# Gate and up projections by a seven-product (Strassen) form for two of eight pairs of k-tiles per chunk

## The reference, cut to what matters

```python
D_MODEL, SEQ, D_FF = 2048, 256, 5632
def swiglu(h, w_gate, w_up, w_down):
    return (jax.nn.silu(h @ w_gate) * (h @ w_up)) @ w_down
x = x + 0.5 * swiglu(rmsnorm(x, ffn1_norm), ffn1_w_gate, ffn1_w_up, ffn1_w_down)
...   # input projection, HGRN2, sparse attention, output projection, cross attention
x = x + 0.5 * swiglu(rmsnorm(x, ffn2_norm), ffn2_w_gate, ffn2_w_up, ffn2_w_down)
out = rmsnorm(x, final_norm)
```

## Time and profile before

| | |
|---|---|
| median of 3 runs | 2023.91 us (2022.93 to 2025.12) |
| profiled execution: span | 2022.1 us |
| TensorE busy | 2005.9 us, 99% of the span, 10238 matmuls |
| VectorE busy | 1105.0 us, 55% |
| ScalarE busy | 947.7 us, 47% |
| HBM read | 373.14 MB, 186 GB/s over the span |

### The profile page before, as it was taken

The page is one execution under the profiler, slowest core; times in us unless marked ns, Lnnn a source line. Parts: engine busy times, 40 slices in busy tenths (PEclk is TensorE's granted clock), DMA queues, the critical chain, the costliest instruction groups (busy, mean ns, idle before and its releaser), DMA issues.

```text
span 2022.1 us, 26565 instructions
## 1 busy us (share of the span) xinstructions
PE 2005.9 (99%) x10238; PEld 1657.0 (82%) x10238; DVE 1105.0 (55%) x1394; ACT 947.7 (47%) x1201; POOL 13.6 (1%) x19
## 2 busy tenths in 40 slices
PE   9999999999999999999999999999999999999998
PEld 7888888888888888878777888888888888888886
DVE  5544544445445546766658675644454544444444
ACT  6444444444454444455555564644444444444443
POOL 0000000000000000000002000000000000000000
PEclk9999999999999999999999999999999999999999
DMA  8666666666666556665433465566666666655564
GB/s 300 192 188 189 185 192 190 187 188 212 213 194 190 191 175 209 185 188 164 135 125 117 167 202 163 166 189 190 192 188 188 187 189 190 210 189 195 192 195 146
DMA packets 198859, 376.32 MB, mean 186 GB/s; under 512 B 13312, under 2 KB 19712, under 8 KB 198656
## 3 DMA queue, kind: packets, MB, share of 16 engines
q1 hardware_dynamic: 196960, 374.51, 60.4%
q10 hardware_dynamic: 1824, 0.77, 0.1%
HBM read 373.14 MB, written 2.10 MB: 186 GB/s over the span
## 4 chain that ended last, share of the span: by engine, by line
PE 96%; ACT 2%; DVE 1%; DMA 1%; issue 0%; SPq 0%; DVEq 0%; ACTq 0%
PE psum L1558 90%; PE psum L1581 2%; PE psum L1769 1%; PE psum L1812 1%; PE psum L1570 1%; ACT w_hi L518 0%; DVE w_lo L967 0%; DMA w_raw<-in_g 0%; ACT prob L759 0%; PE psum L1782 0%; PE psum L1867 0%; DMA w_raw<-in_w_in 0%; PE psum L1791 0%; ACT silu_gate L759 0%; PE psum L1805 0%
## 5 line engine op out<-in xcount | busy, mean ns | idle before, releaser
L967 DVE TENSOR_TENSOR w_lo<-w_raw,w_hi 128x1024 fp32r<-128x1024 f32 x694 | 848.4, 1225 | 868.4 <-ACT w_hi L518 866.5
L518 ACT ACTIVATE w_hi<-w_raw 128x1024 fp32r<-128x1024 f32 x694 | 734.5, 1060 | 993.3 <-PE psum L1558 969.9
L1558 PE MATMUL psum<-w_hi,xT_hi 128*128 128x512 f32 (+1 forms) x1824 | 712.6, 391 | 1.5 <-DVE w_lo L1084 1.3
L1558 PE MATMUL psum<-w_hi,xT_lo 128*128 128x512 f32 (+1 forms) x1824 | 707.6, 388 | 0.0
L1558 PE MATMUL psum<-w_lo,xT_hi 128*128 128x512 f32 (+1 forms) x1824 | 707.0, 388 | 0.0
L1558 PEld LDWEIGHTS psum<-w_hi,xT_hi 128*128 128x128 f32 x1824 | 342.5, 188 | 71.5 <-issue 1.6
L1558 PEld LDWEIGHTS psum<-w_hi,xT_lo 128*128 128x128 f32 x1824 | 342.4, 188 | 70.8
L1558 PEld LDWEIGHTS psum<-w_lo,xT_hi 128*128 128x128 f32 x1824 | 342.7, 188 | 68.2
L1558 PE MATMUL psum<-w_hi,ffT_hi 128*128 128x512 f32 x784 | 306.4, 391 | 0.0
L1558 PE MATMUL psum<-w_hi,ffT_lo 128*128 128x512 f32 x784 | 305.2, 389 | 0.0
L1558 PE MATMUL psum<-w_lo,ffT_hi 128*128 128x512 f32 x784 | 305.0, 389 | 0.0
(11 more groups left out here) (250 smaller groups left out, 864.8 us busy)
## 6 DMA issues: line engine op xcount, KB each, us to landing
w_raw<-in_u SPq DMA_DIRECT2D x176, 512.0 KB, 3.7
w_raw<-in_d SPq DMA_DIRECT2D x176, 512.0 KB, 4.4
w_raw<-in_g SPq DMA_DIRECT2D x175, 512.0 KB, 3.7
w_raw<-in_w_in SPq DMA_DIRECT2D x88, 512.0 KB, 3.7
w_raw<-in_w_out SPq DMA_DIRECT2D x32, 512.0 KB, 3.6
w_raw<-in_cw SPq DMA_DIRECT2D x8, 512.0 KB, 3.7
w_raw<-in_wk SPq DMA_DIRECT2D x8, 512.0 KB, 4.6
w_raw<-in_wq SPq DMA_DIRECT2D x8, 512.0 KB, 3.6
```

The costliest lines, as they stand in the source:

```text
L518: nc.scalar.activation(w_hi[:, slot], w_raw[:, slot], ACT.Copy).then_inc(w_hi_ready, 1)
L967: nc.vector.tensor_tensor(w_lo[:, slot], w_raw[:, slot], w_hi[:, slot].bitcast(F32), ALU.subtract)\
L1558: mm = nc.tensor.matmul(dst[:, t, 0:width], act_t, w[:, slot, kk, 0:width], start=(first and kk == 0 and n == 0), stop=(last and kk == KT_ ...
```

## The change

**Which products.** In chunks 1 to 10 of each half-step, k-tiles 0, 1 and k-tiles 2, 3 are taken as pairs. With the two token tiles as rows, the two k-tiles as the inner dimension and (gate, up) as columns, a pair is a 2 x 2 by 2 x 2 product of blocks, 8 block products of 3 matmuls each. It is now done by 7 block products (Winograd's variant of Strassen's form). That needs four sums of token blocks (`s_hi`, `s_lo`, made once in each half-step by `token_forms`) and, for each pair and chunk, three sums of weight blocks (`t_f32`, then `t_hi`, `t_lo`) and a fourth that is written over `w_raw`.

**Order.** A unit is now one k-tile with both gate and up columns (the input is laid out anew for this, `gu1`, `gu2`), so that all four of banks 0 to 3 are open through the whole chunk. The pairs are units 0, 1 and 6, 7 (`PAIR_AT`). The first unit of a pair is four block products into banks 4, 6, 7, 5, the second is three block products into banks 0, 1, 2. The other 12 units are 12 matmuls as before (`both_unit`).

**Gathering.** After unit 7 ScalarE copies bank 4 (`p1_copied`) and VectorE combines banks 5 to 7 in three additions into `comb` (`combined`). At the chunk's end VectorE adds banks 0, 1 and then 2, 3 to `comb` (`c_taken`, L1274 of the changed kernel), ScalarE takes silu in `comb`, and VectorE writes the product (`hid_ff`). The transposes of the product before now follow unit 12 (`TURN_H`).

**Memory.** `t_f32`, `t_lo`, `t_hi` and `hid_ff` lie in the memory of `x`. In the first half-step `x` is loaded again from the input during the first down chunk, in four transfers of 512 KB (`X_BACK`); in the second it is first written to a buffer in HBM by ScalarE's queue (`x_save`, 2 MB) and loaded back in the same way. The loads of `mem` and of the final norm's rows move to later positions of the down projection.

```diff
+PAIRS = ((0, 1), (2, 3))
+PAIR_AT = (0, 6)
+W_KT = [0] * KD
+for _i, _p in enumerate(PAIR_AT):
+    W_KT[_p], W_KT[_p + 1] = PAIRS[_i]
+_rest = [p for p in range(KD) if p not in PAIR_AT and p - 1 not in PAIR_AT]
+for _kt, _p in enumerate(_rest):
+    W_KT[_p] = 2 * len(PAIRS) + _kt
+U_CH = KD
+MID_EV = PAIR_AT[-1] + 1
...
+        t_f32 = nc.alloc_sbuf_tensor_at("t_f32", [P, 3, NW], F32, offset=x_at)
+        t_lo = nc.alloc_sbuf_tensor_at("t_lo", [P, 3, NW], F32R, offset=x_at)
+        t_hi = nc.alloc_sbuf_tensor_at("t_hi", [P, 3, NW], F32R, offset=x_at + 6144)
+        hid_ff = nc.alloc_sbuf_tensor_at("hid_ff", [P, NT, NW], F32, offset=x_at + 12288)
...
+        comb = nc.alloc_sbuf_tensor_at("comb", [P, 4, NW], F32, offset=ang_at)
+        s_sum = nc.alloc_sbuf_tensor_at("s_sum", [P, 2, 2, NT, P], F32, offset=ang_at + 4096)
...
+        s_hi = nc.alloc_sbuf_tensor_at("s_hi", [P, 4, 2, P], F32R, offset=keep)
+        s_f32 = nc.alloc_sbuf_tensor_at("s_f32", [P, 4, 2, P], F32, offset=keep + 4096)
+        s_lo = nc.alloc_sbuf_tensor_at("s_lo", [P, 4, 2, P], F32R, offset=keep + 4096)
...
+                    for p in range(U_CH):
+                        load(u0 + U_CH * ch + p, (u0 + p) % SLOTS, both(w, W_KT[p], ch))
...
+                        if n == 0 and j in X_BACK:
+                            i = X_BACK.index(j)
+                            if i == 0:
+                                sp.wait_ge(unit_done, u0)
+                                sp.wait_ge(turned, b_h + FF_CHUNKS)
+                                if u0 == U_DN2:
+                                    sp.wait_ge(x_saved, 16)
+                            sp.dma_start(x[:, :, i * NW:(i + 1) * NW],
+                                         src[:, i * NW:(i + 1) * NW].rearrange("(t p) n -> p t n", p=P))\
...
+                if q in PAIR_AT:
+                    act.wait_ge(t1_ready, n_pair)
+                    split(u, slot, turn_no)
+                    return
+                split(u, slot, turn_no)
+                act.wait_ge(t_ready, n_pair)
+                nc.scalar.activation(t_hi[:], t_f32[:], ACT.Copy).then_inc(t_hi_ready, 1)
...
+                                act.dma_start(x_save.rearrange("(t p) n -> p t n", p=P), x[:]).then_inc(x_saved, 16)
...
+                def body(ch, ending):
+                    for p in range(U_CH):
+                        split_ahead(u0, ch, p, not (ending and p + SLOTS >= U_CH))
+                        if p == MID_EV:
+                            act.wait_ge(unit_done, u0 + U_CH * ch + MID_EV + 1)
+                            act.wait_ge(h_ready, base_c + ch)
+                            nc.scalar.activation(comb[:, 0, :], psum[:, 4, :], ACT.Copy).then_inc(p1_copied, 1)
+                        if p == TURN_H + 1:
+                            take(b_h - 1 + ch, 0, ffT_hi, (ch - 1,))
+                    for t in range(NT):
+                        act.wait_ge(c_taken, 2 * base_c + 2 * ch + t + 1)
+                        last = nc.scalar.activation(comb[:, 2 * t, :], comb[:, 2 * t, :], ACT.Silu,
+                                                    scale=rstd[:, norm, t:t + 1])
+                    last.then_inc(gate_ready, 1)
...
+                if q not in PAIR_AT:
+                    split(u, slot)
+                    dve.wait_ge(t_hi_ready, n_pair)
+                    nc.vector.tensor_tensor(t_lo[:], t_f32[:], t_hi[:].bitcast(F32), ALU.subtract).then_inc(t_lo_ready, 1)
+                    return
+                next_slot = (slot + 1) % SLOTS
+                b11, b12, b21, b22 = (w_raw[:, x_, g, :] for x_ in (slot, next_slot) for g in range(2))
+                t3, t2, t4 = (t_f32[:, n, :] for n in range(3))
+                if not opening:
+                    dve.wait_ge(unit_done, u0 + U_CH * ch + PAIR_AT[i - 1] + 2)
+                dve.wait_ge(w_loaded[slot], 16 * turn_no)
+                dve.wait_ge(w_loaded[next_slot], 16 * ((u0 + p + 1) // SLOTS + 2 + U_CH // SLOTS * ch))
+                nc.vector.tensor_tensor(t3, b22, b12, ALU.subtract)
+                nc.vector.tensor_tensor(b12, b12, b11, ALU.subtract).then_inc(t1_ready, 1)
+                dve.wait_ge(t1_ready, n_pair)
+                nc.vector.tensor_tensor(t2, b22, b12, ALU.subtract).then_inc(t2_ready, 1)
+                dve.wait_ge(t2_ready, n_pair)
+                nc.vector.tensor_tensor(t4, b21, t2, ALU.subtract).then_inc(t_ready, 1)
+                split(u, slot)
+
...
+                    last = products(hid_ff, lambda t: pair[1][:, t, :], lambda t: sg[:, t, :])
+                    last.then_inc(h_ready, 1)
+                    nc.vector.memset(taken_mark[:], 0.0).then_inc(c_taken, 2)
...
+                        if p == MID_EV:
+                            dve.wait_ge(unit_done, u0 + U_CH * ch + MID_EV + 1)
+                            dve.wait_ge(p1_copied, (FF_CHUNKS - 1) * nth + ch)
+                            nc.vector.tensor_tensor(comb[:, 2, :], psum[:, 5, :], comb[:, 0, :], ALU.add).then_inc(combined, 1)
...
+                    dve.wait_ge(combined, base_e + 3 * ch)
+                    dve.wait_ge(unit_done, u0 + U_CH * ch + U_CH)
+                    for t in range(NT):
+                        c2 = comb[:, 2 * t:2 * t + 2, :]
+                        nc.vector.tensor_tensor(c2, psum[:, 2 * t:2 * t + 2, :], c2, ALU.add).then_inc(c_taken, 1)
...
+                    last = products(hid_ff, lambda t: comb[:, 2 * t + 1, :], lambda t: comb[:, 2 * t, :])
...
+            def both_unit(u, slot, kt, opens, last):
+
+                pe.wait_ge(w_lo_ready, u + 1)
+                for t in range(NT):
+                    for g in range(2):
+                        mm = product(2 * t + g, *tokens(kt, t), w_hi[:, slot, g, :], w_lo[:, slot, g, :],
+                                     opens and 2 * t + g == 3, last)
+                mm.then_inc(unit_done, 1)
+
...
+                pe.wait_ge(w_lo_ready, u + 1)
+                product(4, *tokens(ka, 0), *half(slot, 0), first, last)
+                product(6, *form(0), *half(slot, 1), first, last)
+                pe.wait_ge(t_lo_ready, n_pair)
+                product(7, *form(2), *made(0), first, last)
+                product(5, *form(1), *made(1), first, last).then_inc(unit_done, 1)
+                pe.wait_ge(w_lo_ready, u + 2)
+                if first:
+                    pe.wait_ge(c_taken, taken - 1)
+                product(0, *tokens(kb, 0), *half(nxt, 0), first, False)
+                product(1, *form(3), *half(nxt, 1), first, False)
+                if first:
+                    pe.wait_ge(c_taken, taken)
+                product(2, *tokens(kb, 1), *made(2), first, False).then_inc(unit_done, 1)
+
...
+                    pe.wait_ge(s_lo_ready, nth + 1)
+                    pe.wait_ge(gate_ready, base_c + 1)
+                    if b_h:
+                        pe.wait_ge(turn_lo, b_h)
...
+                            pe.wait_ge(p1_copied, (FF_CHUNKS - 1) * nth + ch)
+                            pe.wait_ge(combined, 3 * (FF_CHUNKS - 1) * nth + 3 * ch - 2)
+                            pe.wait_ge(h_ready, base_c + ch)
+                            batch(b_h - 1 + ch, 0, lambda j, t: hid_ff[:, t, j * P:(j + 1) * P], False)
+                    pe.wait_ge(combined, 3 * (FF_CHUNKS - 1) * nth + 3 * ch)
+                    pe.wait_ge(turn_lo, b_h + ch)
+
...
+        "gu1": np.stack([inputs[f"ffn1_w_{w}"][0].reshape(D, FF_CHUNKS, NW) for w in ("gate", "up")], 2).reshape(D, -1),
```

268 lines of the change are left out of this document (179 added, 89 removed).

## The result

| | before | after |
|---|---|---|
| median | 2024.45 us (2022.93 to 2025.12, 4 runs) | 2042.68 us (2042.05 to 2042.77, 4 runs) |
| span of the profiled execution | 2022.1 us | 2040.9 us |
| ratio | | 1.0092, 95% interval 1.0077 to 1.0106 |

The change makes the kernel slower by 0.9%, 18.8 us of span; 12.0 were forecast, and the measured time lies in the range.

The account below looks back on a forecast made before the run. TensorE, busy 99% of the span, was taken to set the end. Matmuls -27.2, chunk ends +20.0, last chunk ends +11.2, first chunk ends +5.0, clock +3.0 make +12.0 on 2023.9: 2036 us, range 2026 to 2050.

Parts of the forecast that it names:

- 120 matmuls, 27.2 us: Ten chunks in each half-step, two pairs each, three matmuls fewer per pair, at 0.227 us: 27.2 us less.
- 18 x 1.11 at the chunk ends: Nine chunk ends per half-step: TensorE waits for VectorE's addition to free bank 0, 1.11 us each, 20.0 us.
- bank 4, which `ffT_lo` frees, comes 0.30 after T with the restart: Chunk end: TensorE gets bank 4 0.30 us after T, when the next unit's first matmul would start; restart 0.17.
- The last chunk ends, 11.2: Before each half-step's down projection TensorE waits for two additions and silu: 2 x 5.6 = 11.2 us.
- The clock, 3.0: After the two 5.6 us waits TensorE's clock falls; cost between nothing and 3.1 us each, 1.5 taken, 3.0 in all.
- the late VectorE: First rival: VectorE later than counted, 0.5 us more per chunk end, clock's upper bound, x write; 2050 us, chance 0.19.
- The first chunk ends, 5.0: First chunk of each half-step: TensorE loses 3.7 us in the first, 1.25 in the second, together 5.0.
- `token_forms` (some 4 us of VectorE) falls into units 8 to 10 of the first chunk, where that engine idles 1.5 us in each unit: nothing: First chunk: making the token sums fits into VectorE's idle time and costs nothing.
- Traffic, nothing: Reloads of x, moved loads and the 2 MB write of x are covered: nothing, at worst 2 us for the write.
- The rival in which the wait for bank 0 is missing: At chunk ends the first addition finishes in time, the 20.0 us vanish; 2016 us, chance 0.07.
- The losses are partly covered: Second rival: clock stays up, chunk-end delays are 0.9 us; sum +3, 2027 us, no change that can be told; chance 0.12.
- another pace: Rival: four banks in turn instead of two might change the 0.227 us per matmul; given no chance of its own.

Follow-up runs that it names:

- all repairs: Changed kernel with banks 0 to 3 added before unit 19, ffT_hi/ffT_lo before unit 17, reordered opening, first down unit waiting for c_taken only: 2001.83 us, ratio 0.9892.
- the filling of the waits: Changed kernel with 22 useless matmuls put into TensorE's wait before the first down unit of each half-step: 2038.98 us, ratio 1.0077.
- the first experiment: Changed kernel with VectorE adding banks 0 to 3 to comb before it makes unit 19's w_lo: 2030.15 us, ratio 1.0035.
- the other opening: Changed kernel, each half-step's first chunk: token sums' parts one step later, product and mark earlier, no gate wait in the first half-step: 2035.28 us, ratio 1.0059.

## Why the prediction was right, point by point

- **120 matmuls, 27.2 us.** Right, and the pace of four banks in turn is 0.2268 us as before: 43.07 a chunk with all repairs. (The Trainium skill, "TensorE: Matmul & The Clock Gate", section "Back-to-back issue gap", has two figures for 512 columns: N / 2.4 + 2.5 ns, about 216, for the gap of single matmuls, which is the one that the prediction took, and about 131 ns for a stream in which each matmul has its weight load, as here. By the first a chunk would be an estimated 2 us shorter, by the second some 18. The traces agree with neither for these matmuls.)
- **18 x 1.11 at the chunk ends.** The total was right (1.13 to 1.19), the reasons only in part. The step "bank 4, which `ffT_lo` frees, comes 0.30 after T with the restart" took the restart of 0.17 from the earlier trace rows, where a unit's own wait stands directly ahead of its matmul. Here the wait stands ahead of the loop's branch, and bank 4 costs 0.86. Bank 0 then costs 0.33 and not 0.81, because the two do not add: the later wait ends at a fixed time after T. Without the weight sums the loss was 1.13 by the other wait alone. That is why the total came out right with a wrong part, and why the repair of bank 0 alone brought so little. There is luck in it: the later wait hid the mistake only because 0.86 is less than 1.11.
- **The last chunk ends, 11.2.** Right to 0.1, since each step had a row for it. Silu in `comb` takes 0.72 and not 0.62; against that, the restart's slow first matmul is counted in the clock's row here.
- **The clock, 3.0.** The mechanism was right, the size was little more than half of what it is. "I take the middle, 1.5 each" had no ground beyond being between 0 and 3.1; what happened lay near the upper end, read from the warm-up (2.6 and 3.0, of which the filling of the waits gave back 5.3). (The Trainium skill, the same page, section "HAM oscillation — how this bites in real kernels", has the clock thrown back by a wait of some 3 to 5 us before each group: the traces agree for the waits of 3.3 us and more. The gaps of 0.8 us and less at the chunk ends are shorter than those and left the clock up.) Had the clock fallen at the chunk ends too, it would have been the first rival, the late VectorE, that grew; the prediction names the second.
- **The first chunk ends, 5.0.** The failed step is "`token_forms` (some 4 us of VectorE) falls into units 8 to 10 of the first chunk, where that engine idles 1.5 us in each unit: nothing". It is true of VectorE. But ScalarE must make `s_hi` in between, in order, and so waits for VectorE's sums (3.20 us) with its weight copies behind it. The variance's square root, placed at 49.6, came at 52.64 and the silus, placed at 53.8, at 56.82. That, and the clock at half pace, which the sum counted only at the down projections, turn 3.7 into 7.7. How much is ScalarE's order and how much a wait for `gate_ready` that guards nothing was not tried apart.
- **Traffic, nothing.** Right as far as it was tried: without the write of `x` there is no gain. For the loads there is only the absence of waits for weights.
- **The rivals.** A VectorE that is too busy falls with the run without weight sums and with that of all repairs, which keeps the sums and has no wait in a chunk. The rival in which the wait for bank 0 is missing named a real wait (the first experiment takes it away), but priced it too high: bank 4's 0.86 would have been left. "The losses are partly covered" and "another pace" fall.

Of the 6.8 us by which the forecast was short, 2.6 are the clock, 2.9 the openings, 0.9 the chunk ends, and 0.3 stand in no row. The same wait of 5.5 us costs the clock more or less according to how early in it the clock falls: 4.2 and 5.0 us after TensorE stopped in the changed kernel, about 2.2 in the run with the other opening. It also matters how soon the clock comes back: behind the second wait of the run without the write it did so 3.4 us after the fall and not 6.8. What stays open is why it falls, or comes back, sooner in one execution than in another.

## What to carry to other kernels

Fewer operations on the engine that sets the end gain only what the hand-over leaves: once all accumulators end together, the evacuation of the first one wanted must stand ahead of everything else on the evacuating engine, and each wait must be for that evacuation and not for the last step of its chain. When two late releases follow each other closely, repairing the later one shows only what it adds to the earlier; find the first late one and mend from there. And price a gap on TensorE with what it does to the clock afterwards: here a quarter to a half of its length again, from 3.3 us on.
